# Two-layer diffusion step on one core: first copies of the second product on ScalarE, high parts in front of low ones, scale loaded in front of the weights

## What is computed

```python
for layer in range(2):
    mod_p = ada_params(c_ctx[None, :], w_mod[layer], b_mod[layer])   # shift, scale, gate, shift, scale, gate
    mod_s = ada_params(c, w_mod[layer], b_mod[layer])
    hp = modulate(rmsnorm(xp, norm_mix_pre[layer]), mod_p[0], mod_p[1])
    hs = modulate(rmsnorm(xs, norm_mix_pre[layer]), mod_s[0], mod_s[1])
    ...                                   # even layer: gMLP and RG-LRU mixer; odd layer: windowed attention
    hp = modulate(rmsnorm(xp, norm_ffn_pre[layer]), mod_p[3], mod_p[4])
    xp = xp + mod_p[5] * rmsnorm(square(relu(hp @ w_ffn_in[layer])) @ w_ffn_out[layer], norm_ffn_post[layer])
    ...                                   # the same for xs
```

## Time and profile before

| | |
|---|---|
| median of three runs | 1427.66 us |
| profiled execution | 1429.37 us, span 1427.3 us |
| TensorE matmul busy | 1373.6 us (96%) |
| VectorE, ScalarE, GpSimd busy | 62%, 49%, 50% |
| mean granted TensorE clock | 0.988 of full |

### The profile page before, as it was taken

The page is one execution under the profiler, slowest core; times in us unless marked ns, Lnnn a source line. Parts: engine busy times, 40 slices in busy tenths (PEclk is TensorE's granted clock), DMA queues, the critical chain, the costliest instruction groups (busy, mean ns, idle before and its releaser), DMA issues.

```text
span 1427.3 us, 20872 instructions
## 1 busy us (share of the span) xinstructions
PE 1373.6 (96%) x7682; PEld 1162.0 (81%) x7682; DVE 885.5 (62%) x1543; ACT 706.2 (49%) x1431; POOL 715.1 (50%) x547
## 2 busy tenths in 40 slices
PE   5999999989999999999999989999899999999998
PEld 3876787868888888989767867788789899899896
DVE  4477864866655565565663578627855655656646
ACT  4375824744434444443552367637544534444443
POOL 1430413775445556555352567635855565555550
PEclk8999999999999999999999999999999999999999
DMA  9534272533454412212455200034323222231213
GB/s 350 161 95 142 69 257 68 192 118 119 136 209 157 148 59 90 89 62 87 153 185 185 89 2 1 1 118 172 108 90 104 74 91 87 72 106 59 89 60 148
DMA packets 98059, 164.32 MB, mean 115 GB/s; under 512 B 11100, under 2 KB 49704, under 8 KB 97960
## 3 DMA queue, kind: packets, MB, share of 16 engines
q1 hardware_dynamic: 86320, 157.23, 32.4%
q10 hardware_dynamic: 11640, 5.76, 1.6%
HBM read 154.82 MB, written 8.16 MB: 114 GB/s over the span
## 4 chain that ended last, share of the span: by engine, by line
PE 45%; DVE 2%; POOL 2%; issue 1%; ACT 0%; DVEq 0%; POOLq 0%; ACTq 0%
PE PS L2025 13%; PE PS L2026 13%; PE PS L2027 13%; PE PS L2367 2%; PE PS L2356 1%; PE PS L2335 1%; PE PS L2075 1%; PE PS L2336 1%; PE PS L2319 0%; PE PS L2312 0%; POOL WLU L1592 0%; POOL GG L1538 0%; PE PS L2115 0%; POOL HL L1561 0%; DVE HF L1786 0%
## 5 line engine op out<-in xcount | busy, mean ns | idle before, releaser
L1592 POOL TENSOR_TENSOR WLU<-RAW,WHU 128x512 fp32r<-128x512 f32 x340 | 457.5, 1371 | 376.3 <-ACT WHU L1227 376.2
L1227 ACT CAST WHU<-RAW 128x512 fp32r<-128x512 f32 x340 | 197.3, 618 | 236.9 <-PE PS L2027 121.7
L2025 PE MATMUL PS<-WHU,MXR 128*128 128x512 f32 x640 | 254.6, 398 | 11.9 <-issue 9.8
L2026 PE MATMUL PS<-WLU,MXR 128*128 128x512 f32 x640 | 252.0, 394 | 0.0
L2027 PE MATMUL PS<-WHU,MXR 128*128 128x512 f32 x640 | 251.6, 393 | 0.0
L1934 DVE TENSOR_TENSOR ACC<-ACC,PS 128x512 f32<-128x512 f32 x260 | 177.6, 684 | 94.8 <-PE PS L2027 93.7
L1587 POOL TENSOR_TENSOR WL<-RAW,WH 128x512 fp32r<-128x512 f32 x84 | 117.5, 1432 | 212.9 <-ACT WH L1218 195.4
L2025 PE MATMUL PS<-HH,WHU 128*128 128x320 f32 (+2 forms) x576 | 178.8, 310 | 3.9 <-POOL HL L1561 3.9
L2027 PE MATMUL PS<-HH,WLU 128*128 128x320 f32 (+2 forms) x576 | 178.6, 310 | 0.0
L2026 PE MATMUL PS<-HL,WHU 128*128 128x320 f32 (+2 forms) x576 | 178.5, 310 | 0.0
L2025 PEld LDWEIGHTS PS<-WHU,MXR 128*128 128x128 f32 x640 | 121.1, 189 | 47.2 <-issue 17.9
(11 more groups left out here) (274 smaller groups left out, 2637.3 us busy)
## 6 DMA issues: line engine op xcount, KB each, us to landing
RAW<-in_w_ffn_in SPq DMA_DIRECT2D x32, 1024.0 KB, 5.5
RAW<-in_w_ffn_out SPq DMA_DIRECT2D x32, 1024.0 KB, 5.0
RAW<-in_w_mod SPq DMA_DIRECT2D x18, 1024.0 KB, 5.8
GG<-in_w_mod SPq DMA_DIRECT2D x13, 1024.0 KB, 7.4
MX<-in_w_mod SPq DMA_DIRECT2D x11, 1024.0 KB, 5.2
RAW<-in_w_in_even SPq DMA_DIRECT2D x7, 1024.0 KB, 5.3
RAW<-in_w_qkv SPq DMA_DIRECT2D x6, 1024.0 KB, 7.5
xd<-X SPq DMA_DIRECT2D x10, 512.0 KB, 8.0
```

What stands on the lines that cost most here:

```text
L1227: nc.scalar.copy(unit_view(WHU, u), unit_raw(u["ld"], u["of"])).then_inc(u_hi, 1)
L1592: nc.gpsimd.tensor_tensor(unit_view(WLU, u), unit_raw(u["ld"], u["of"]), unit_view(WHU, u).bitcast(f32), ALU.subtract)\
L2025: MM(out, wh, xh, start=first, stop=False, skip_group_check=reopens)
L2026: MM(out, wh, xl, start=False, stop=False, skip_group_check=reopens)
```

## The change

There are four edits.

1. At kernel begin the two loads of the scale's first half are put in front of the load of the first weight block. The three places in memory (`EARLY`) go by number of load, so the scale's two parts now land in `MX` and the weights in `GG`.
2. The first `N` of part 1 (pair 0, f 0) issues its 16 matmuls with the high inputs first and waits for the high parts alone (`f_hi`); its 8 matmuls with the low inputs follow and wait for the low parts.
3. The ten copies of the groups of pair 0 are made by ScalarE, in both layers.
4. The unit (2, S3) is given a place of at least `NS + 8` (it was `NS + 5`), and with it all units behind it in `order` that stood close.

```diff
+                if o == (2, "S3"):
+                    at = max(at, NS + 8)
...
     mod(0, 0, 0)
+    scale_ld = mod_load(0, 1, 0)
     ld = load("acols", src=("w_in",), col=1536)
...
-    mod(0, 1, 0)
+    mod(0, 1, 0, scale_ld)
...
+                elif k == "g" and not s["p"]:
+                    b = s["b"]
+                    act.wait_ge(t_add, 12 * s["layer"] + 12)
+                    upto(act, b_ready, b)
+                    nc.scalar.copy(ACC[:, s["t"], 512 * s["nh"]:512 * s["nh"] + 512], PS[:, 4 + b % 2, :]).then_inc(b_free[b % 2], 1)
...
-                elif k == "g":
+                elif k == "g" and s["p"]:
                     b, acc = s["b"], ACC[:, s["t"], 512 * s["nh"]:512 * s["nh"] + 512]
                     upto(dve, b_ready, b)
...
-                        V_.tensor_copy(acc, PS[:, 4 + b % 2, :]).then_inc(b_free[b % 2], 1)
...
+                    if (p, f, part) == (0, 0, 1):
+                        cols = DIRECT[1]
+                        for i in (0, 1):
+                            u = s["units"][i]
+                            pe.wait_ge(u_lo, u["number"] + 1)
+                            pe.wait_ge(f_hi[i], TT * layer + 5)
+                            for kt in range(4):
+                                for w in (WHU, WLU):
+                                    MM(out, unit_view(w, u)[:, kt, :], HH[:, 4 * i + kt, cols], start=w is WHU and (i, kt) == (0, 0), stop=False)
+                        for i in (0, 1):
+                            u = s["units"][i]
+                            pe.wait_ge(f_lo[i], TT * layer + 5)
+                            for kt in range(4):
+                                ins = MM(out, unit_view(WHU, u)[:, kt, :], HL[:, 4 * i + kt, cols], start=False, stop=(i, kt) == (1, 3))
+                        ins.then_inc(n_done, 1)
+                        continue
```

More of the change, by code:

```diff
@@ L1927, in _ @@
                     V_.tensor_copy(QS[:, i % 2, :], m_bank(u)).then_inc(m_free[u % 2], 1)
-                elif k == "g":
+                elif k == "g" and s["p"]:
                     b, acc = s["b"], ACC[:, s["t"], 512 * s["nh"]:512 * s["nh"] + 512]
                     upto(dve, b_ready, b)
[L1931 to L1935, removed]
-                        V_.tensor_copy(acc, PS[:, 4 + b % 2, :]).then_inc(b_free[b % 2], 1)
+                    V_.tensor_tensor(acc, acc, PS[:, 4 + b % 2, :], ALU.add).then_inc(b_free[b % 2], 1)
                 elif k == "G2":
@@ L2178, in _ @@
                         pe.wait_ge(n_read, DIRECTS[layer, p, f, 0])
-                    if p == 0 and f == 0:
+                    out = direct_bank(s)
+                    if (p, f, part) == (0, 0, 1):
[14 more added lines that the diff above has]
+                        continue
+                    if (p, f) == (0, 0):
                         for half in (0, 1):
-                            pe.wait_ge(f_lo[half], TT * layer + (2, 5)[part])
-                    out = direct_bank(s)
+                            pe.wait_ge(f_lo[half], TT * layer + 2)
                     for i in (0, 1):
```

## The result

The changed kernel takes 1431.97 us in the median of 20 runs; the kernel before, run beside it, 1428.97 us. The ratio is 1.002, 95% interval 1.0014 to 1.0026: slower by 2.9 us (2.0 to 3.7). The interval leaves out no change, though the size is just the 0.2% that the prediction took as the least that can be told. A second set (10 runs against 27) gave 1.0029 (1.0017 to 1.004), 4.1 us. The forecast was 1.2 us slower. The profiled execution of the first set took only 1428.37 us; it is the fastest of its 20, so its total must not be read as the kernel's. What it shows stretch by stretch can. One timed run of the twelve experiments, of the changed kernel without its edit at kernel begin, took 2487 us and is left out of that kernel's median.

A forecast was written before the change was run, and what follows sets the result against it. TensorE, busy 96% of the span, was taken as the bound. Begin 0, layer 0 -0.7, layer 1 +0.3 and clock +1.6 gave +1.2 on the 1427.66 us median: 1428.9, range 1422.0 to 1433.0.

The forecast's parts named there:

- High parts first and copies on ScalarE: Pair 0 of the feed-forward: P1 comes 4.0 us earlier in layer 0 (3.5 to 6.0), 3.0 in layer 1 (2.5 to 5.0).
- The step behind it: Pair 0: all ten copies stand behind comb1's cast, ScalarE won't be earlier, so TensorE idles 4.3 us before group 3.
- The new stall: Pair 1, groups 6 and 7: VectorE's sum S3 waits for A22's low part; 3.3 us in each layer (2.6 to 3.9).
- the count of units: Behind S3 of pair 2: the fourth edit was said to move the fifteen-odd units behind it as well.
- Rival 1: Pair 1: the new stall doesn't come, engines behind P1 have more slack; -7.0 us, 1420.7 (about 1424 with half); chance 0.22.
- The clock behind the stall: TensorE behind the new stall: lower clock costs 0 to 2.5 us in each layer; 1.6 taken for one of the two.
- The two rows I bounded it by: First product of part 1: a 2.01 us wait left the clock at 1.00 in layer 0; in layer 1 0.55 followed.
- Kernel begin: A0: 0.85 us of waiting for low parts goes, a later clock rise may lose net 0.7; taken as 0.
- a sign of being wrong: Kernel begin: A0 was to stay at 34.1 without gaps; the prediction is wrong if A0 itself moves.
- rival 2: Sum S3 of pair 3, both layers: stall 3.3 to 3.9 plus 1.6 lower clock each, A0 slower; +3.5, 1431.2; chance 0.30.
- the case I held likeliest: Whole kernel: gain and new stall about cancel, +1.2 us to 1428.9, own range 1426 to 1431; chance 0.42.
- Rival 3: Pair 0: the clock stays full through the 4.3 us wait for comb1; -4.4 us, 1423.3; chance 0.06.

## Why the prediction was right, and where its sizes were off

**High parts first and copies on ScalarE: P1 4.0 and 3.0 us earlier.** Right. From the first product of part 1, with the wait in front of it, P1 took 43.6 us before in layer 0. In the three traces with the feed-forward's whole change it took 39.6, 39.8 and 39.1: 4.1 less. In layer 1 it took 42.5 before, then 38.8, 40.2 and 39.0: 3.2 less. The second trace without the change (the run with kernel begin alone) had 42.6 and 42.5; with the mean of both the gain in layer 0 is 3.6. The step behind it held in detail: the first copy right behind `comb1`, 4.4 us of idling before group 3 (4.3 forecast), none before group 8. That `comb1` doesn't move with TensorE was shown by the run without high parts first: there TensorE's first product of part 1 came 3.45 us later than in the changed kernel's trace (274.19 against 270.74), of which 1.29 us had been lost before that place (GpSimd's low parts begin at 269.27 against 267.98), and `comb1` began just 1.28 us later (296.21 against 294.93). In every trace but one (layer 1 of the run with the copies left on VectorE) `comb1` begins 22.3 us after these low parts end.

**The new stall: 3.3 us in each layer.** Right in place, cause and size. A22's low part was forecast 22.0 after P1; the sum that waits for it began 332.07 - 310.30 = 21.8 after. The sum took 1.67 us instead of 1.18, and the addition was done at 24.6 instead of 24.4. GpSimd's start, forecast 17.7 after P1, came at 17.7. Only the count of units was wrong: nine moved with S3, not fifteen-odd, and the chain didn't rest on it. Rival 1 (the stall doesn't come) is refuted. Of the two groups that my chain had waiting, 6 and 7, only group 6 does; group 7 began 26.6 to 27.4 after P1 (forecast 26.5), later by what group 6 took.

**The clock behind the stall: +1.6 once.** This term was mis-sized. From P1 to the next P1 layer 0 took 29.1 us before (344.44 - 315.36) and 33.8 in the changed kernel (344.06 - 310.30); 34.2 and 33.6 in the two other traces; layer 1 went from 29.1 to between 33.5 and 33.8. Of these 4.4 to 5.1 us the wait explains 3.4; 1.0 to 1.7 is the lower clock, in each of the layers and in all three traces: 2.5 for the two layers together, where I had 1.6. The two rows I bounded it by, 2.0 us with and without a loss, were right as bounds; the wait was 3.26 us, not the 2.5 I gave it, and nearer to the 4 us rows that were always followed by 1.2 GHz. It isn't certain at 3.26 either: in layer 1 of the run without high parts first the clock stayed full behind it.

**Kernel begin: 0.** Right in sum: 1.0 (0.9992 to 1.0009) alone. Both parts of it are in that run's trace: A0's wait for low parts is gone, and the block still takes 5.00 us (33.98 to 38.98) instead of 4.47, at the lower clock until 37.0. In the changed kernel's trace A0 began at 33.51, not 34.10, which I had named as a sign of being wrong. Its loads had come 0.5 us earlier than in the run with kernel begin alone (29.02 against 29.49), with the same order of loads, so the edit doesn't explain it.

**The sum.** With the measured terms: -4.1 - 3.2 for P1, +4.8 + 4.6 for the stalls with their clock, 0 for the begin: +2.1, or +2.6 with the -3.6 of both traces without the change. The forecast had +1.2, the two ratios say +2.9 and +4.1. Every term of the forecast came where it was put, but the lower clock behind the stall came in both layers and not in one. That is rival 2's case: stall and clock, 9.4 us, exceed the 6.8 to 7.3 that P1 gains, and its +3.5 lies nearer to the two ratios than the forecast's +1.2. Its lower clock at A0 came too, but cost nothing net. So the time fell into the stated range by the right mechanism, while the case I held likeliest was not quite the one that came: 1431.97 is 1 us above that case's own range of 1426 to 1431. Of the 3.1 us between it and my 1428.9, 1.3 is the base, since the kernel before took 1428.97 in the larger set and not 1427.66. Rival 3 is refuted: the clock fell in the 4.4 us wait. Some 0.3 to 2 us between the sum and the ratios stay open, since the runs without a trace can't be looked into.

**What I didn't see.** I took high parts first as a gain that goes into the next wait at no cost. It made one long wait out of two shorter ones, and the clock behind it made that cost 3 to 4 us in all.

## What to carry to other kernels

Count a late step from what it waits for at the far end: the placement of one unit in pair 0 cost more in pair 1 than ten copies gave, by its effect on the nine units behind it, and one step less would have cost nothing. When work is moved off a waiting queue, move only what waits there: the first two copies were fine where they were. And a gain that ends in a longer wait is not zero but negative, if that wait grows long enough for the clock to fall.

## What was not expected of the hardware

Two waits of TensorE of 2.0 and 2.2 us, some 24 us apart, left the clock at full speed in layer 0, while one of 4.3 to 4.4 us was followed by 1.2 GHz in all five traces that have it, in both layers, for 3.4 or 6.8 us of which up to 2.5 lay in the wait itself. In between, the length of a single wait doesn't tell: 1.86 to 1.91 us before the first product of part 1 was followed by 1.2 GHz in layer 1 of three traces, 2.01 us at the same place in layer 0 of the same traces was not, and 3.25 to 3.27 us was in nine places of ten.

Waits that the order of the queues sets repeated from one execution to the next within 0.05 us (3.25 to 3.27 in these ten places), while whole executions of one kernel differed by 6.5 us (1428.37 to 1434.84). The mean granted clock doesn't tell the two kernels apart: 0.9886 for the changed kernel at 1429.9 us of mean span, 0.9887 for the one before at 1427.4. So about as much time goes at 1.2 GHz in both, behind other waits, and the 2.5 us between the means are idle time in the main; how much exactly isn't shown.
